# A two-layer decoder trunk with eight experts: experts grouped in five teams, longer weight runs, a modulation sum shared with TensorE

## The reference, cut to what matters

```python
cond = jax.nn.silu(c)
for l in range(DEPTH):                      # DEPTH = 2
    mod = cond @ ada_w[l] + ada_b[l]        # 1024 x 6144: six modulation vectors
    h = rmsnorm(x, norm1_g[l]) * (1.0 + sc1) + sh1
    x = x + g1 * (mix(h @ w_in[l]) @ w_out[l])
    h = rmsnorm(x, norm2_g[l]) * (1.0 + sc2) + sh2
    x = x + g2 * (swiglu(h, ...) if l % 2 == 0 else moe_swiglu(h, ...))
# moe: top-2 of 8, weights softmaxed; out += w * ((silu(x_b @ wg[e]) * (x_b @ wu[e])) @ wd[e])
```

## Time and profile before

| what | value |
| --- | --- |
| median of 3 runs | 1687.45 us (1686.11 to 1691.96) |
| the profiled execution | 1692.91 us, span 1691.1 us |
| PE busy in the span | 1611.1 us (95%) |
| mean granted TensorE clock | 0.977 |
| DMA | 481.53 MB, mean 285 GB/s |

### The profile page before, as it was taken

One profiled execution on the slowest core, in us unless ns is written; L12 is line 12 of the kernel. 1 busy time (PEld: TensorE's weight loads), 2 busy tenths in 40 slices (PEclk: granted clock), 3 DMA queues, 4 the chain that ended last, 5 costly groups with the idle time before them and its releaser, 6 DMA issues.

```text
span 1691.1 us, 16145 instructions
## 1 busy us (share of the span) xinstructions
PE 1611.1 (95%) x6482; PEld 868.2 (51%) x6482; DVE 480.8 (28%) x953; ACT 199.0 (12%) x439; POOL 0.9 (0%) x7
## 2 busy tenths in 40 slices
PE   3999989999989999789999999999999999999997
PEld 2566755555546667554454444454444444444443
DVE  6577733434343644330110011100111000111002
ACT  1123230000011233200010000000000000000000
POOL 0000000000000000000000000000000000000000
PEclk9999899999999999789999999999999999999999
DMA  9935625888762100099999998999999989999993
GB/s 347 327 109 199 236 87 174 277 294 290 286 233 96 58 1 1 1 345 395 392 368 391 392 392 332 387 341 389 388 359 370 386 337 389 392 359 361 392 392 125
DMA packets 222010, 481.53 MB, mean 285 GB/s; under 512 B 15816, under 2 KB 33608, under 8 KB 221936
## 3 DMA queue, kind: packets, MB, share of 16 engines
q1 hardware_dynamic: 220488, 478.64, 76.8%
q10 hardware_dynamic: 1448, 1.84, 0.5%
HBM read 479.41 MB, written 1.06 MB: 284 GB/s over the span
## 4 chain that ended last, share of the span: by engine, by line
PE 91%; DMA 3%; DVE 2%; SPq 2%; ACT 1%; issue 1%; DVEq 0%; ACTq 0%
PE bank L1209 31%; PE bank L1238 16%; PE bank L1204 11%; PE bank L971 7%; PE bank L1230 6%; PE bank L962 4%; PE bank L1178 3%; PE bank L1216 2%; DMA ring<-in_ada_w 1%; DMA ring<-in_moe_wg 1%; PE bank L1284 1%; PE bank L1300 1%; PE bank L1098 1%; DVE ada_acc L1412 1%; PE bank L952 1%; SPq L607 1%
## 5 line engine op out<-in xcount | busy, mean ns | idle before, releaser
L1209 PE MATMUL bank<-ring,h_T 128*128 128x512 f32 (+1 forms) x896 | 355.3, 550 | 3.8 <-ACT h_T L727 1.3
L1238 PE MATMUL bank<-ring,m_qk_T 128*128 128x512 f32 x624 | 277.7, 597 | 0.7 <-ACT m_qk_T L843 0.7
L1209 PEld LDWEIGHTS bank<-ring,h_T 128*128 128x128 f32 x896 | 167.8, 191 | 165.2 <-issue 114.7
L1209 PE MATMUL bank<-ring,cmp_region 128*128 128x512 f32 x448 | 197.1, 593 | 0.0
L1238 PEld LDWEIGHTS bank<-ring,m_qk_T 128*128 128x128 f32 x624 | 116.2, 190 | 144.8 <-issue 140.9
L1763 DVE SCALAR_TENSOR_TENSOR m_s_region<-s_v,bank 128x512 f32<-128x512 f32 (+1 forms) x70 | 39.1, 558 | 489.8 <-ACT s_v L836 353.2
L836 ACT ACTIVATE s_v<-bank 128x512 f32<-128x512 f32 (+1 forms) x70 | 34.5, 493 | 997.5 <-PE bank L1209 654.1
L1209 PEld LDWEIGHTS bank<-ring,cmp_region 128*128 128x128 f32 x448 | 83.7, 190 | 99.6 <-issue 99.6
L1767 DVE SCALAR_TENSOR_TENSOR m_s_region<-m_s_region,bank 128x512 f32<-128x512 f32 (+1 forms) x70 | 39.1, 558 | 317.6 <-PE bank L1209 224.3
L971 PE MATMUL bank<-ring,h_T 128*128 128x512 f32 (+1 forms) x320 | 117.6, 517 | 0.0
L1204 PE MATMUL bank<-ring,h_T 128*64 128x256 f32 x896 | 102.4, 381 | 1.0 <-DVE m_s_region L1767 1.0
(11 more groups left out here) (314 smaller groups left out, 1022.0 us busy)
## 6 DMA issues: line engine op xcount, KB each, us to landing
ring<-in_moe_wg SPq DMA_DIRECT2D x56, 2048.0 KB, 9.7
ring<-in_moe_wu SPq DMA_DIRECT2D x56, 2048.0 KB, 15.5
ring<-in_moe_wd SPq DMA_DIRECT2D x56, 2048.0 KB, 19.1
ring<-in_ada_w SPq DMA_DIRECT2D x28, 1024.0 KB, 8.9
ring<-in_ada_w SPq DMA_DIRECT2D x10, 2048.0 KB, 14.4
ring<-in_w_in SPq DMA_DIRECT2D x10, 2048.0 KB, 12.1
ring<-in_ffn_wg SPq DMA_DIRECT2D x6, 1536.0 KB, 10.4
ring<-in_ffn_wu SPq DMA_DIRECT2D x6, 1536.0 KB, 9.4
```

Of the source, the lines that this page charges most:

```text
L1209: last = mm(ps[4 + part][:, 0:w], xT[st.into][:, k, 128 * st.tile:128 * st.tile + 128], view_at(slot, w)[:, k, :], start=k == 0, stop=k == ...
L1238: last = mm(ps[st.y + half][:, :], hbT[:, j % 2, 128 * q:128 * q + 128], down_at(st.slots[2], st.w)[:, q, 512 * half:512 * half + 512], st ...
```

## The change

Experts are ranked as before but placed in five teams with capacities 96 + 32, 128, 96 + 32, 128 and 64 + 64 (ranks 2, 7; 0; 3, 6; 1; 4, 5). A team is one tile of 128 rows; its members use columns of the array side by side, each as one lane of 128 or lanes of at most 64 columns, so a 96-row member is a lane of 64 and a lane of 32, and a 32-row member a lane of 32. Per team the hidden columns are worked in stages of 2, 2, 2 and 1 units. In a stage of 2 a load of `wg` or `wu` is 512 rows by 1024 columns (runs of 4 KB); a load of `wd` puts two adjacent rows in one partition (runs of 8 KB, the transposes take every second column to match). SP's loop over pairs is written out. Scatters use weighted one-hots, so the four adds of a team are plain additions. OVER is 4. In the head, k = 4..7 of the first four chunks are multiplied on TensorE with `cond` broadcast over 128 columns, straight into the bank that the ones product adds to, and the result is taken by a diagonal mask and a sum.

```diff
-HALF = 64
-OVER = 3
+OVER = 4
+TEAMS = (((0, 0, 96), (1, 96, 128)), ((2, 0, 128),), ((3, 0, 96), (4, 96, 128)), ((5, 0, 128),), ((6, 0, 64), (7, 64, 128)))
+SLOT_RANK, SLOT_CAP = (2, 7, 0, 3, 6, 1, 4, 5), (96, 32, 128, 96, 32, 128, 64, 64)
+SPANS = ((0, 2), (1024, 2), (2048, 2), (3072, 1))
+class Stage:
+    def __init__(self, team, s, at):
...
+        self.lanes = [(m, a, min(a + (128 if c1 - c0 == 128 else 64), c1)) for m, (_, c0, c1) in enumerate(TEAMS[team])
+                      for a in range(c0, c1, 128 if c1 - c0 == 128 else 64)]
...
+    for j in range(len(STAGES) + 1):
+        if j < len(STAGES):
+            for part in range(2):
+                for piece in range(STAGES[j].units):
+                    add(STAGES[j], part, piece)
+        if j:
+            for unit in range(STAGES[j - 1].units):
+                add(STAGES[j - 1], 2, unit)
...
@@ SP
-            with sp.Fori(0, PAIRS) as i:
-                pair = [sp.value_load(orderi[0:1, bass.ds(i * 2 + q, 1)], min_val=0, max_val=N_EXP - 1) for q in range(2)]
-                for u in range(7):
-                    for q in range(2):
-                        for j in range(3):
-                            expert_load(6 * u + 3 * q + j, pair[q], u, j, i * 6)
+            for n, (st, part, piece, m) in enumerate(MOE_LOADS):
+                e, slot = expert_id(st.team, m), n % RING
+                sp.wait_ge(ring_free[slot], FREED[slot] + n // RING)
+                if part == 2:
+                    f0 = st.f0 + 512 * piece
+                    sp.dma_start(ring[:, slot, :].rearrange("p (g n) -> p g n", g=2),
+                                 w[f0:f0 + 512, :].rearrange("(g p f) n -> p g (f n)", p=128, f=2)).then_inc(ring_full[slot], 16)
+                elif st.units == 2:
+                    sp.dma_start(wide_at(slot), w[512 * piece:512 * piece + 512, st.f0:st.f0 + 1024].rearrange("(k p) n -> p k n", p=128)).then_inc(ring_full[slot], 16)
+                else:
+                    sp.dma_start(view_at(slot, 512), w[:, st.f0:st.f0 + 512].rearrange("(k p) n -> p k n", p=128)).then_inc(ring_full[slot], 16)
...
@@ PE
+            def ada_half_product(c):
+                i, b = AT[(0, "ada", c)], ada_bank(0, c)
+                loaded(pe, i)
...
+                for k in range(KC // 2, KC):
+                    mm(b[:, :], cond[:, k:k + 1].to_broadcast([128, 128]), w[:, k, :], start=k == KC // 2, stop=False)
...
+            def moe_up(j, part, between=None):
...
+                for piece in range(2):
+                    if piece < st.units:
+                        moe_loaded(pe, st, part, piece)
+                    for unit in range(st.units):
+                        b = ps[((4, 2), (5, 3))[part][unit]]
+                        for k in range(4 * piece, 4 * piece + 4):
+                            for n, (m, c0, c1) in enumerate(st.lanes):
...
+                                last = mm(b[c0:c1, :], xT[st.team % 2][:, k, c0:c1], w, start=k == 0, stop=k == KC - 1)
...
+            def moe_down(j):
...
+                    for half in range(2):
+                        for q in range(4):
+                            for n, (m, c0, c1) in enumerate(st.lanes):
+                                slot = moe_slot(st, 2, unit, m)
+                                last = mm(ps[half][c0:c1, :], hbT[:, unit, 128 * q + c0:128 * q + c1],
+                                          down_at(slot, 512)[:, q, 512 * half:512 * half + 512],
+                                          start=st.begin and unit == 0 and q == 0, stop=end and q == 3)
...
+            for j in range(len(STAGES) + 1):
+                if j < len(STAGES):
+                    moe_up(j, 0, between)
+                    moe_up(j, 1)
...
+                if j:
+                    moe_down(j - 1)
...
@@ DVE
+            def ada_half_sum(c):
+                do(TS(a, w[:, 0, :], cond[:, 0:1], None, ALU.mult))
+                for k in range(1, KC // 2):
+                    do(STT(a, w[:, k, :], cond[:, k:k + 1], a, ALU.mult, ALU.add), acc_ready if k == KC // 2 - 1 else None)
...
+                elif l == 0 and c < 4:
+                    do(TTop(diagonal, b[:, :].rearrange("p (q n) -> p q n", q=4), eye, ALU.mult), mod_evac)
+                    do(V.tensor_reduce(modc[:, 4 * c:4 * c + 4], diagonal, AX.X, ALU.add))
+                    do(TTop(modc[:, 4 * c:4 * c + 4], modc[:, 4 * c:4 * c + 4], prm(l, "ada_b")[:, 4 * c:4 * c + 4], ALU.add))
...
+            def add_team(team, n, bank=7):
+                do(TTop(xs, ps[bank][:, :], xs, ALU.add), moe["added"])
```

More of the change, by code:

```diff
@@ L270, with __init__ @@
 class Step:
-    def __init__(self, w, tile, y, loads, rounds, first, last, begin, end, half=False, into=0):
+    def __init__(self, w, tile, y, loads, rounds, first, last, begin, end):
         self.w, self.tile, self.y, self.loads, self.rounds = w, tile, y, loads, rounds
         self.first, self.last, self.begin, self.end = first, last, begin, end
-        self.half, self.ew, self.into = half, w // 2 if half else w, into
         self.slots = [n % (PRE if rounds is None else RING) for n in loads]
@@ L1200, in up @@
                     for k in range(KC):
[L1201 to L1210, removed]
+                        last = mm(ps[4 + part][:, 0:w], hT[:, k, 128 * st.tile:128 * st.tile + 128], view_at(slot, w)[:, k, :],
+                                  start=k == 0, stop=k == KC - 1)
                     last.then_inc(f["gu"[part]], 1)
@@ new lines, in moe_scatter @@
+            def moe_scatter(team, n, bank=7, added=True):
+                half, tt = divmod(n, 2)
+                pe.wait_ge(moe["y_1" if half else "y_0"], team + 1)
+                if n == 0:
+                    pe.wait_ge(moe["turn_evac"], team + 1)
+                if added and n:
+                    pe.wait_ge(moe["added"], 4 * team + n)
+                mm(ps[bank][:, :], pickT[team % 2][:, tt, :], ysb[:, 512 * half:512 * half + 512],
+                   start=True, stop=True).then_inc(moe["scattered"], 1)
@@ new lines, in _, with between @@
+            for j in range(len(STAGES) + 1):
+                def between(piece):
+                    if j and piece < STAGES[j - 1].units:
+                        moe_turn(j - 1, piece)
+                    beside(j, piece)
+                if j < len(STAGES):
+                    moe_up(j, 0, between)
+                    moe_up(j, 1)
+                    beside(j, 2)
+                else:
+                    moe_turn(j - 1, 0)
+                if j:
+                    moe_down(j - 1)
+                if j < len(STAGES):
+                    beside(j, 3)
@@ L1777, in picks_turned, with onehot @@
-            def picks_turned(f, n, count, do):
+                    doe(TS(pick[0][:, tt, :], cst("iota"), over_rank[:, tt, bass.ds(e, 1)], None, ALU.is_equal), over["onehot"] if tt else None)
+            def onehot(team):
+                for tt in range(TT):
+                    for at, c0, c1 in TEAMS[team]:
+                        do(TS(pick[0][:, tt, c0:c1], cst("iota")[:, 0:c1 - c0], rank[:, tt, at:at + 1], None, ALU.is_equal),
+                           moe["onehot"] if team == 0 and tt and c1 == 128 else None)
@@ L1808, in add_residual, with add_over @@
+            def add_over(half, column, count):
+                dve.wait_ge(over["scattered"], count)
+                for tt in range(TT):
+                    xs = x[:, tt, 512 * half:512 * half + 512]
+                    doe(STT(xs, ps[(2, 7)[tt]][:, :], wts[:, tt, bass.ds(column, 1)], xs, ALU.mult, ALU.add), over["added"] if tt else None)
             def add_residual(tt, half, y):
```

427 lines of the change are left out of this document (256 added, 171 removed).

## The result

The changed kernel takes 1938.96 us (median of 4, 1937.31 to 1941.83) against 1689.7 us for the kernel before in the same session (median of 4, 1686.11 to 1693.83). The ratio is 1.1476, with a 95% interval of 1.1442 to 1.151: slower by 14.8%. The forecast was 1930 us. The case that it held likeliest, with a chance of one half, is the one that came.

The account below looks back on a forecast made before the run. TensorE was taken to lead, transfers following closely. Experts at 1203.5 us, 250 more than before, and -7.5 around them gave a 1933.6 us span, 1930 us on the median's scale; own range 1895 to 1965, 8 in 10 from 1632 to 1965.

Parts of the forecast that it names:

- What bounds, and the price of a product: Experts before the change: TensorE leads, transfers follow closely; a full group of 8 products takes 6.87 us.
- The step of three lanes: Each k of a 96 + 32 team: 64-wide lane 1.00 us, then two 32-wide lanes together 0.98, in all 1.98 us.
- (a): Rival for the experts: 64- and 32-column lanes overlap, two-expert teams follow the bytes; 1646 us in all; chance 0.40.
- The teams: Expert teams in order: 340, 155, 344, 155 and 190 us, with 7 for the last down product.
- 12.5 us for the first piece: Start of the experts: 12.5 us until two slots have landed, 10.3 of bytes and 2.2 for issue and landing.
- The bytes: Expert weight loads: 8 KB runs at 421 GB/s, bounds 409 and 434; 858 us of transfers for all experts.
- Around the experts: Outside the experts: head -2 us, router order -0.5, end -5, together -7.5 us.
- The sum: Experts 1203.5 us, 250 more than before, and -7.5 around them: a span of 1933.6 us.
- break-even step: Three-lane step of the 96 + 32 teams: below 1.27 us, over 2 teams x 168 steps, the change would gain.
- (b): Rival on TensorE: records of different lanes start strictly in program order, 1.29 us for three lanes; 1697 us; chance 0.06.
- (c): Rival: one more assignment sends an expert into the overflow loop, at least 145 us on top of (a), 1790; chance 0.02.
- (d): Rival: lanes cost something between and gains cancel, within 5 us of now; chance 0.02.

Follow-up runs that it names:

- equal lanes: Changed kernel with all lanes of the 96 + 32 teams 32 columns wide: 1653.11 us, ratio 0.9777 to the kernel before.
- unequal ones in another order: Changed kernel, unequal lanes kept, but per piece of 4 k all products of the 64-wide lane first, then the 32-wide ones: 1870.14 us, ratio 1.1068.
- The head alone: Kernel before with only the first four modulation sums made half by TensorE products: 1686.69 us, ratio 0.9979.
- with 2 KB runs: Equal lanes with down loaded in 4 KB runs and gate and up in 2 KB runs, one unit per stage: 1677.8 us, ratio 0.9915.

## Why the prediction was right, point by point

**What bounds, and the price of a product.** TensorE led before, and the six-record step was priced from the spacing of starts. Both hold: the one-expert teams have the 155 us that were worked out from 21 groups of 6.87 us and the extras (155 and 155 us in the windows of the equal lanes, where no products of a slower team run over into them).

**The step of three lanes.** Predicted 1.98 us, 1.00 for the 64-wide lane and 0.98 for the two 32-wide ones; measured 1.985, 1.00 and 0.98. The evidence for it was thin: one hand-over between tiles of 64 and 32 rows, while nothing in the trace spoke of columns. The reading of that row holds up: the hand-over takes the same 0.31 us in head h = 0 (139.02 to 139.33 us), where L1038's rows lie inside L1035's tile and can't run beside it. But rows were taken for columns, and with chances of 0.50 against 0.40 the choice over (a) was close to a toss; that it fell right is in part luck. The runs settle what the trace of before could not: equal lanes take 0.86 us per k, unequal ones in another order 1.78. So it is neither the number of lanes nor that of records; three quarters of the added time are missing overlap (0.86 of 1.12 us per k), the rest the changes. The Trainium skill, in "TensorEngine Tiling (Array Packing)", Key Properties, has a change of tiling mode drain TensorE, and the page's list of configurations has 128x64 and 128x32 as two. The traces of this case agree, with 1.985 us per k for mixed widths against 0.86 for equal ones.

**The teams.** The first 96 + 32 team with the one-expert team behind it takes from 731.25, its first product, to 1224.6 us, 493.4 us, against 340 + 155 = 495; the second pair 501.3 against 499. They can only be compared together, since the last products of a two-expert team run inside the next team. The 12.5 us for the first piece were 12.8. The last team takes 202.8 us instead of 197, the largest error of the sum. Under 2 of these 6 us are seen: its last group of down products takes 8.78 us, where a group of that size takes 7.09 at full clock, with 2.12 us of idle time ahead of it and a mean granted clock of 0.81. In the middle of that team such a group should cost nothing, since the bytes lead; no run isolates that. The other 4 us stay open.

**The bytes.** 8 KB runs were estimated at 421 GB/s, between 409 and 434; measured 419, in equal lanes. In the changed kernel itself little hung on it, since TensorE leads there.

**Around the experts.** The head was to bring 2 us and the order 0.5; together they brought 3.8. The head alone, on the kernel before, brings 1.7 us at the first load in its profiled execution and 3.5 (1.7 to 5.4) by the ratio. How the 3.8 divide can't be told: with equal lanes the first load is issued at 716.03 us in one execution and at 714.35 in another, and over the profiled executions of all kernels that have both changes it lies between 713.25 and 719.89. The end was to bring 5 us and brought 3.9.

**The sum.** 1203.5 - 7.5 was predicted for experts and surroundings, 1210.4 - 7.7 measured. The span was to be 1933.6 and is 1940.0 us. Two side figures of the prediction don't come out of its own terms. Its break-even step is 1.26 us (961.3 less 519.5 for all that isn't a 96 + 32 team and 18.8 for these teams' extras, over 336 steps), not 1.27. And (a) at 409 or 434 GB/s for down gives some 1652 and 1639 us, not 1670 and 1630. The forecast rests on neither.

**The rivals.** (a), that unequal columns overlap, was priced at 1646 us. It isn't so; but a kernel in which the lanes are equal is just that case, and it takes 1653 us, 7 us above. Some 4 of these are scale: (a) counts from 1687.45 us for the kernel before, whose median beside the equal lanes was 1691.15. In the profiled execution the experts take 1640.1 - 716.0 = 924.1 us against 920. The terms can be read in the windows: two-expert teams at the rate of the bytes, one-expert teams at 155 us. (b), strict order of records, would make four slots of 0.43 us for each k of four lanes, 13.8 us for a group, where 7.07 are measured. (c), overflow, didn't occur: the trace has 56 loads each of `wg`, `wu` and `wd`, the 168 of the eight experts and none more. (d), cancelling gains, falls with the step.

**A version that beats both.** The equal lanes: 0.9777 of the kernel before, and 1653.11 / 1938.96 = 0.853 of the changed one. So teams, long runs, head and end together are worth 38 us; the one unequal width in the list of lanes had turned them into a loss of 249.

## What to carry to other kernels

When experts or heads share TensorE's array side by side, cut all of them to one width, the smallest that is needed: four lanes of 32 columns take 7.07 us per group where one of 128 takes 7.03, while a 64-wide lane with two 32-wide ones takes 2.3 times as long (1.985 us per k against 0.86). Where a trace has no row for the new combination, price it from both ends and say which row decides; then the first thing to try is the smallest edit that removes the doubtful property, here one line. Check after such a gain which resource now leads, since the next microseconds are found only there: with equal lanes the bytes lead, and 4 and 8 KB runs instead of 2 and 4 KB are worth 26 us.

## What the runs showed of the hardware

Tiles of 64 and 32 columns in disjoint columns of the array don't run beside each other (1.985 us per k); each change costs 0.13 us with the first weights, some 0.09 without. Tiles of equal width do, four of 32 (7.07 us for 8 k) as well as two of 64 (7.09). Runs of 2, 4 and 8 KB move at 387, 409 and 419 GB/s in loads of 2 MiB.

Less expected was the clock in a stage that the bytes lead. With equal lanes TensorE's mean granted clock is 0.92 in the first team, where it is 0.99 in the same team of the changed kernel, since part of the products behind a wait for bytes run at the lower level of 1.2 GHz. Groups behind gaps of 2.70 and 2.12 us take 8.78 us, groups behind 0.45 and 1.55 us take 7.09 and 7.07. The gap just ahead doesn't decide it alone: with 2 KB runs the last down group, behind 2.44 us, takes 7.09 us at a granted clock of 1.00. Where such a group stands at the very end the lower level adds 1.7 us.
